# Two transformer blocks on one core: the second block's joints by halves, a shorter opening, one early turn

## What is computed

```python
def rms_norm(x, gain):
    y = x * lax.rsqrt(jnp.mean(x * x, axis=-1, keepdims=True) + NORM_EPS)
    return y * gain

def swiglu_2(h, w_in, w_out):
    g, u = jnp.split(h @ w_in, 2, axis=-1)
    return (jax.nn.silu(g) * u) @ w_out

def second_block(x, ...):
    for layer in range(2):
        g = norm_gain[layer]
        h = swiglu_2(rms_norm(x, g[0]), ffn_w_in[layer, 0], ffn_w_out[layer, 0])
        x = x + 0.5 * rms_norm(h, g[1])
        h = token_mixer(rms_norm(x, g[2]), ...)
        x = x + rms_norm(h, g[3])
        h = swiglu_2(rms_norm(x, g[4]), ffn_w_in[layer, 1], ffn_w_out[layer, 1])
        x = x + 0.5 * rms_norm(h, g[5])
    return x
```

## Time and profile before

| | |
|---|---|
| median of 3 runs | 2106.71 us (2106.12 to 2107.46) |
| the profiled execution | 2107.18 us |
| its span, first to last instruction | 2105.4 us |
| TensorE busy in it | 99% |
| VectorE, ScalarE busy | 80%, 51% |
| DMA moved | 395.56 MB, 188 GB/s |
| granted clock of TensorE | 1.00 |

### The profile page before, as it was taken

The page is one execution under the profiler, slowest core; times in us unless marked ns, Lnnn a source line. Parts: engine busy times, 40 slices in busy tenths (PEclk is TensorE's granted clock), DMA queues, the critical chain, the costliest instruction groups (busy, mean ns, idle before and its releaser), DMA issues.

```text
span 2105.4 us, 28912 instructions
## 1 busy us (share of the span) xinstructions
PE 2093.0 (99%) x10580; PEld 1777.1 (84%) x10580; DVE 1685.9 (80%) x3158; ACT 1082.8 (51%) x1568; POOL 87.0 (4%) x128
## 2 busy tenths in 40 slices
PE   9999999999999999999999999999999999999998
PEld 7888999888888899988878888988888888888887
DVE  5888766888888877778888887779889888678886
ACT  5445553544544455444454446575445445666443
POOL 0000010000000000000000001010000000101000
PEclk9999999999999999999999999999999999999999
DMA  7765755666566584557656767446665765645663
GB/s 243 237 195 173 225 163 161 190 213 197 178 218 195 170 240 146 185 168 226 195 153 212 218 190 196 124 137 209 211 196 171 223 192 169 185 141 162 211 191 106
DMA packets 314368, 395.56 MB, mean 188 GB/s; under 512 B 17972, under 2 KB 272212, under 8 KB 313972
## 3 DMA queue, kind: packets, MB, share of 16 engines
q1 hardware_dynamic: 309120, 375.52, 58.1%
q0 software_dynamic: 4944, 18.14, 2.8%
q10 hardware_dynamic: 164, 0.06, 0.0%
HBM read 392.59 MB, written 1.06 MB: 187 GB/s over the span
## 4 chain that ended last, share of the span: by engine, by line
PE 95%; DVE 2%; ACT 1%; issue 1%; POOL 0%; DMA 0%; DVEq 0%; POOLq 0%; SPq 0%; ACTq 0%
PE bank L310 26%; PE bank L312 26%; PE bank L311 26%; PE bank L304 4%; PE bank L305 4%; PE bank L306 4%; PE bank L491 1%; DVE w_lo L294 1%; PE bank L1472 1%; PE bank L1493 1%; PE bank L1001 1%; PE bank L1564 1%; DVE x L805 0%; ACT w_hi L287 0%; ACT xt_hi L834 0%
## 5 line engine op out<-in xcount | busy, mean ns | idle before, releaser
L287 ACT ACTIVATE w_hi<-stage 128x1024 fp32r<-128x1024 f32 x711 | 747.0, 1058 | 636.3 <-PE bank L312 530.6
L294 DVE TENSOR_TENSOR w_lo<-stage,w_hi 128x1024 fp32r<-128x1024 f32 x711 | 865.5, 1223 | 215.8 <-ACT w_hi L287 208.7
L310 PE MATMUL bank<-w_hi,xt_hi 128*128 128x512 f32 x1760 | 691.4, 393 | 1.7 <-DVE w_lo L621 1.5
L312 PE MATMUL bank<-w_hi,xt_lo 128*128 128x512 f32 x1760 | 685.5, 389 | 0.0
L311 PE MATMUL bank<-w_lo,xt_hi 128*128 128x512 f32 x1760 | 685.2, 389 | 0.0
L477 DVE STREAM_TRANSPOSE hidden<-hidden 32x128 f32<-32x128 f32 (+1 forms) x1376 | 391.7, 285 | 21.3
L310 PEld LDWEIGHTS bank<-w_hi,xt_hi 128*128 128x128 f32 x1760 | 330.5, 188 | 70.1 <-DVE w_lo L621 1.7
L312 PEld LDWEIGHTS bank<-w_hi,xt_lo 128*128 128x128 f32 x1760 | 330.4, 188 | 69.3
L311 PEld LDWEIGHTS bank<-w_lo,xt_hi 128*128 128x128 f32 x1760 | 330.6, 188 | 66.3
L310 PE MATMUL bank<-w_hi,mt_hi 128*128 128x512 f32 x768 | 303.2, 395 | 0.6 <-DVE mt_lo L561 0.6
L312 PE MATMUL bank<-w_hi,mt_lo 128*128 128x512 f32 x768 | 299.4, 390 | 0.0
(11 more groups left out here) (279 smaller groups left out, 1396.5 us busy)
## 6 DMA issues: line engine op xcount, KB each, us to landing
stage<-in_ffn_w SPq DMA_DIRECT2D x352, 256.0 KB, 3.2
stage<-in_ffn_w_in SPq DMA_DIRECT2D x352, 256.0 KB, 3.2
stage<-in_ffn_w SPq DMA_DIRECT2D x88, 512.0 KB, 3.7
stage<-in_ffn_w_out SPq DMA_DIRECT2D x88, 512.0 KB, 3.7
stage<-in_w_in SPq DMA_DIRECT2D x80, 512.0 KB, 4.2
stage<-in_mix_w_in SPq DMA_DIRECT2D x56, 512.0 KB, 4.3
stage<-in_w_out SPq DMA_DIRECT2D x16, 512.0 KB, 4.1
stage<-in_mix_w_out SPq DMA_DIRECT2D x16, 512.0 KB, 3.5
```

The source lines that it names most:

```text
L287: act.activation(w_hi[:, u % RING, :], stage[:, u % STAGED, :], ACT.Copy).then_inc(S["hi_ready"], 1)
L294: dve.tensor_tensor(w_lo[:, u % RING, :], stage[:, u % STAGED, :], f32(w_hi[:, u % RING, :]), ALU.subtract).then_inc(S["lo_ready"], 1)
L310: pe.matmul(o, m_hi, hi, start=first, stop=False)
L312: return pe.matmul(o, m_lo, hi, start=False, stop=last)
```

## The change

Six edits:

1. `WARM` goes from 14 to 8.
2. In stage 0 VectorE turns tile 0's hidden step 2 at units 15 and 16 rather than 16 and 17.
3. At the joints from stage 5 on, x of a tile is made by halves, and each half is followed at once by its product with the next norm's row (`dve_pre_half`).
4. Tile 1's half turns in stages 6, 8, 9 and 11 stand behind tile 0's units 5 and 6 rather than both ahead of unit 5. VectorE's order there: the gate first, then x and product by halves, `xt_lo` of half 0, `w_lo` of unit 6, `xt_lo` of half 1.
5. Tile 0's turns into stage 6: half 0 ahead of tile 1's last unit, half 1 behind it; `xt_lo` by halves round the `w_lo`. Into the other stages both stay ahead of the last unit.
6. The variance behind a stage of the second block: the first half sum is scaled early, and one instruction adds the second.

```diff
-WARM = 14
+WARM = 8
...
-            first = [...] if s else [(16, 2, 18, [(0, 2)])]
+            first = [...] if s else [(15, 2, 17, [(0, 2)])]
...
         def pe_ffn(pe, s):
-                if s and v == LAG - 1:
+                if 0 < s < BLOCK2 and v == LAG - 1:
                     pe_turn_x(pe, s, 1)
                 pe_ffn_tile(pe, s, 0, v)
+                if s >= BLOCK2 and v in (LAG - 1, LAG):
+                    pe_turn_half(pe, s, 1, v - LAG + 1)
...
                 if turn and v == n - 1:
-                    pe_turn_x(pe, s + 1, 0)
+                    pe_turn_half(pe, s + 1, 0, 0)
+                    if s + 1 != BLOCK2:
+                        pe_turn_half(pe, s + 1, 0, 1)
                 pe_ffn_tile(pe, s, 1, v)
                 pe_turn_hidden(pe, s, 1, v)
+            if s + 1 == BLOCK2:
+                pe_turn_half(pe, s + 1, 0, 1)
...
         def dve_ffn(dve, s):
                 lo_upto(dve, b + 6)
-                dve_norm_x(dve, s - 1, 1)
-                dve_pre_x(dve, s, 1)
-                dve_gate(dve, s, 0, 0)
-                lo_upto(dve, b + 7)
-                dve_xt(dve, s, 1)
+                if s >= BLOCK2:
+                    dve_gate(dve, s, 0, 0)
+                    dve_norm_x(dve, s - 1, 1)
+                    dve_xt_half(dve, s, 1, 0)
+                    lo_upto(dve, b + 7)
+                    dve_xt_half(dve, s, 1, 1)
+                else:
+                    dve_norm_x(dve, s - 1, 1)
+                    dve_gate(dve, s, 0, 0)
+                    lo_upto(dve, b + 7)
+                    dve_xt(dve, s, 1)
                 if s >= BLOCK2:
                     dve_pre_var(dve, s, 1)
                 lo_upto(dve, b + 9)
...
         def dve_norm_start(dve, s, t, between=lambda: None):
+                factor = post_factor(s)
+                dve.tensor_scalar(var[:, t:t + 1], ss[:, 2 * t:2 * t + 1], factor ** -2 / D, factor ** -2 * NORM_EPS,
+                                  ALU.mult, ALU.add).then_inc(S["post_half"], 1)
...
         def dve_norm_var(dve, s, t):
-                dve.tensor_tensor(ss[:, 2 * t:2 * t + 1], ss[:, 2 * t:2 * t + 1], ss[:, 2 * t + 1:2 * t + 2], ALU.add)\
-                   .then_inc(S["post_sum"], 1)
-                dve.wait_ge(S["post_sum"], post_at(s, t))
-                dve.tensor_scalar(var[:, t:t + 1], ss[:, 2 * t:2 * t + 1], factor ** -2 / D, factor ** -2 * NORM_EPS,
-                                  ALU.mult, ALU.add).then_inc(S["post_var"], 1)
+                dve.scalar_tensor_tensor(var[:, t:t + 1], ss[:, 2 * t + 1:2 * t + 2], post_factor(s) ** -2 / D,
+                                         var[:, t:t + 1], ALU.mult, ALU.add).then_inc(S["post_var"], 1)
...
         def dve_norm_x(dve, s, t):
-                w = D if s + 1 < len(STAGES) else D // 2
-                for c in range(0, D, w):
-                    dve.scalar_tensor_tensor(x[:, t, c:c + w], r[:, t, c:c + w], rstd[:, t:t + 1], x[:, t, c:c + w],
+                for h in range(2):
+                    c = slice(h * 512, (h + 1) * 512)
+                    dve.scalar_tensor_tensor(x[:, t, c], r[:, t, c], rstd[:, t:t + 1], x[:, t, c],
                                              ALU.mult, ALU.add).then_inc(S["x_ready"], 1)
+                    if s + 1 < len(STAGES):
+                        dve_pre_half(dve, s + 1, t, h, rows[:, 1, :])
...
+        def dve_pre_half(dve, s, t, h, gain):
+
+            c = slice(h * 512, (h + 1) * 512)
+            dve.wait_ge(S["x_ready"], x_at(s - 1, t, h))
+            dve.tensor_tensor(xh[:, t, c], x[:, t, c], gain[:, c], ALU.mult).then_inc(S["pre_x"], 1)
```

More of the change, by code:

```diff
@@ L117, in build @@
                   "ln_resid", "ln_mean", "ln_xg", "ln_ss", "ln_var", "ln_rstd", "x_ready",
-                  "post_ss", "post_scaled", "post_sum", "post_var", "post_rstd",
+                  "post_ss", "post_scaled", "post_half", "post_var", "post_rstd",
                   "pre_ss", "pre_var", "pre_rstd", "pre_x", "x_turned", "xt_hi_out", "xt_lo_out"):
@@ L459, in block_turns @@
         def block_turns(s):
-            first = [(8, 2, 10, [(0, 1)]), (10, 2, 12, [(1, 0)])] if s else [(16, 2, 18, [(0, 2)])]
+            first = [(8, 2, 10, [(0, 1)]), (10, 2, 12, [(1, 0)])] if s else [(15, 2, 17, [(0, 2)])]
             both = [(6 * i + 8, 4, 6 * i + 12, [(0, i + 1), (1, i)]) for i in range(1 if s else 2, STEPS - 2)]
@@ L674, in dve_ffn @@
             if s + 1 < len(STAGES):
-                dve_pre_x(dve, s + 1, 0)
-                lo_upto(dve, b + n + 4)
-                dve_xt(dve, s + 1, 0)
+                if s + 1 == BLOCK2:
+                    dve_xt_half(dve, s + 1, 0, 0)
+                    lo_upto(dve, b + n + 4)
+                    dve_xt_half(dve, s + 1, 0, 1)
+                else:
+                    lo_upto(dve, b + n + 4)
+                    dve_xt(dve, s + 1, 0)
                 if scaled_later(s + 1):
@@ L685, in x_at @@
         def x_at(s, t, h):
-            if s < BLOCK2:
-                return 4 * s + 2 * t + h + 1
-            return 4 * BLOCK2 + 2 * (s - BLOCK2) + (t if s + 1 < len(STAGES) else 2 * t + h) + 1
+            return 4 * s + 2 * t + h + 1
         def x_done(s, t):
@@ L763, in act_norm_sq, with post_factor @@
                        .then_inc(S["post_ss"], 1)
+        def post_factor(s):
+            return 1.0 if STAGES[s] == "mix2" else 0.5
         def dve_norm_var(dve, s, t):
@@ L770, in dve_norm_var @@
             else:
-                factor = 1.0 if STAGES[s] == "mix2" else 0.5
+                dve.wait_ge(S["post_half"], post_at(s, t))
                 dve.wait_ge(S["post_ss"], 2 * post_at(s, t))
-                dve.tensor_tensor(ss[:, 2 * t:2 * t + 1], ss[:, 2 * t:2 * t + 1], ss[:, 2 * t + 1:2 * t + 2], ALU.add)\
-                   .then_inc(S["post_sum"], 1)
-                dve.wait_ge(S["post_sum"], post_at(s, t))
-                dve.tensor_scalar(var[:, t:t + 1], ss[:, 2 * t:2 * t + 1], factor ** -2 / D, factor ** -2 * NORM_EPS,
-                                  ALU.mult, ALU.add).then_inc(S["post_var"], 1)
+                dve.scalar_tensor_tensor(var[:, t:t + 1], ss[:, 2 * t + 1:2 * t + 2], post_factor(s) ** -2 / D,
+                                         var[:, t:t + 1], ALU.mult, ALU.add).then_inc(S["post_var"], 1)
                 if last(s, t):
@@ L799, in dve_norm_x @@
                                              ALU.add).then_inc(S["x_ready"], 1)
+                    if s + 1 == BLOCK2:
+                        dve_pre_half(dve, s + 1, t, h, row3)
             else:
@@ L820, in pool_pre @@
                 .then_inc(S["pre_rstd"], 1)
-        def dve_pre_x(dve, s, t):
-            if s < BLOCK2:
-                return
-            gain = row3 if s == BLOCK2 else rows[:, 1, :]
-            dve.wait_ge(S["x_ready"], x_done(s - 1, t))
-            for h in range(2):
-                c = slice(h * 512, (h + 1) * 512)
-                dve.tensor_tensor(xh[:, t, c], x[:, t, c], gain[:, c], ALU.mult).then_inc(S["pre_x"], 1)
+        def dve_pre_half(dve, s, t, h, gain):
+            c = slice(h * 512, (h + 1) * 512)
+            dve.wait_ge(S["x_ready"], x_at(s - 1, t, h))
+            dve.tensor_tensor(xh[:, t, c], x[:, t, c], gain[:, c], ALU.mult).then_inc(S["pre_x"], 1)
         def act_xt_half(act, s, t, h):
```

2 lines of the change are left out of this document (removed).

## The result

| | before | changed |
|---|---|---|
| median of 5 runs | 2107.17 us (2106.12 to 2107.84) | 2125.82 us (2125.32 to 2128.03) |
| profiled execution | 2107.18 us | 2128.03 us |
| its span | 2105.4 us | 2126.3 us |
| granted TensorE clock, mean of the span | 1.000 | 0.995 |

The change makes the kernel slower: ratio 1.0091, 95% interval [1.0081, 1.0102], +18.65 us in the medians where +14.0 was forecast. The profiled execution is the slowest of the five, +20.9 us; the other four have clocks of 0.996 to 0.998 where it has 0.995.

What follows compares the result with a forecast made beforehand. TensorE, busy 2093.0 of 2105.4 us, was taken as the bound. Terms -1.3 - 0.6 - 0.2 + 0.7 + 0.1 + 17.0 - 2.7 + 1.0 = +14.0 us, on the median 2106.71, gave 2120.7 us; range 2114.5 to 2127.0.

Steps and rivals of the forecast that it cites:

- The pauses of tile 1's joints: Stages 6, 8, 9, 11: TensorE stands 2.5 us, then 1.75 us, for VectorE's low weights, four times: +17.0 us.
- a hidden second pause: Rival, tile 1's joints: unit 7's low weights ready within tile 1's unit 0, only first pause remains; 2113.7 us, chance 0.06.
- weights ahead: Rival, tile 1's joints: low weights of units 6 and 7 made before the half turns, no pauses; 2101.9 us, chance 0.05.
- Given back -2.7: Tile 1's joints: the old waits ahead of these turns go, with 0.11 us each inside a pair: -2.7 us.
- new +1.0: Stages 8 and 11: the gate, now ahead of x, waits for a silu; half 0 is 0.5 us late: +1.0 us.
- Tile 0's joints: Into stages 7, 9, 10: x and product by halves make the second half later, +0.23 us each, +0.7.
- the mixers: Tile 1's joints into stages 7 and 10: the shorter variance takes back the split, +0.1 us in all.
- The early turn: Stage 0: tile 0's single turn and mt_lo one w_lo earlier, removing TensorE's wait for mt_lo: -0.6 us.
- the end: Program's end: one 128x1 step less between the last square and the last rstd: -0.2 us.
- The opening: Kernel's start: fewer products on zeros let tile 0's turns and the first weighted product come sooner: -1.3 us.
- the clock rises late in the opening: Rival, opening: the first weighted products run at the lower clock level, 2.1 us more; 2122.8 us, chance 0.07.
- The clock in the pauses: Rival, tile 1's joints: the clock falls in the pauses, 1.6 us a joint, 6.4 in all; 2127.1 us, chance 0.08.

Runs made afterwards that it cites:

- e4: The change plus nine unused identity products behind the hidden turn, filling the first pause in stages 6, 8, 9 and 11: 2123.3 us, +16.3.
- e5: The kernel before with only the change's order of tile 1's half turns and unit 6's low weights, x whole, 14 zeros: 2124.33 us, +18.0.
- e2: The change, but VectorE makes unit 6's low weights ahead of x, with the gate behind x: 2115.88 us, +8.9.
- e7: The kernel before with only the single turn of stage 0 a unit sooner and the new variance form: 2105.75 us, -0.6.
- e6: The kernel before with only WARM 14 to 8 (8 products on zeros): 2106.23 us over 11 runs, -0.1.
- e12: The change with WARM back at 14 (all 14 products on zeros): 2125.62 us, +18.9.
- e3: The change, but low weights of units 6 and 7 made ahead of both xt_lo of tile 1: 2116.36 us, +9.4.
- e10: e3 with ScalarE's square of tile 1's x and VectorE's step on it moved later: 2110.8 us, +4.1.
- e8: e1 with 14 zeros, and tile 0's half 1 low part and squares put behind the units' weights: 2108.36 us, +2.0.
- e11: The change with TensorE's old order alone (both tile 1 half turns ahead of unit 5), VectorE's order as changed: 2118.33 us, +11.6.
- e1: The change with tile 1's half turns and VectorE's order there as before, x and product still by halves: 2108.96 us, +2.0.

## Why the prediction came out as it did

The measured median lies 5.1 us above the forecast's 2120.7 and inside its range; as a difference to before it is +18.65 for +14.0. The terms can be weighed by the distance of two products that stand on both sides of a joint (start us of each, from the timelines; before, the change, and e4, where the upper level held):

| joint | before | change | e4 |
|---|---|---|---|
| both tiles into stage 6 | 1085.14 to 1110.03 | 1083.97 to 1113.24, +4.4 | 1082.91 to 1110.74, +2.9 |
| tile 1 into stage 8 | 1416.23 to 1430.22 | 1419.83 to 1439.37, +5.6 | 1417.32 to 1435.89, +4.6 |
| tile 1 into stage 9 | 1604.22 to 1616.11 | 1613.60 to 1631.32, +5.8 | 1610.16 to 1626.36, +4.3 |
| tile 1 into stage 11 | 1920.06 to 1936.07 | 1935.67 to 1956.98, +5.3 | 1930.63 to 1951.20, +4.6 |
| sum (forecast 15.3) | | +21.1 | +16.4 |

Term by term:

**The pauses of tile 1's joints (+17.0): right.** The first was worked out at 2.5 us and is 2.49, four times; the second at 1.75 and is 1.82 where TensorE ran at the upper level (1.23 and 0.99 in the stages where the lower one had made tile 1's unit 0 longer and ate part of it). e5 shows that the order alone does it, e2 that the two pauses are two, and the rivals that needed a hidden second pause or weights ahead fell. One piece was left out: the first product behind a pause takes 0.34 us to the next one's start and not 0.23 (1615.12 to 1615.46 and 1620.28 to 1620.61 in e4), eight times, 0.9 us. With 0.07 more for each second pause this is the 1.1 us by which e4's joints exceed the forecast's 15.3 (17.0 - 2.7 + 1.0).

**Given back -2.7, new +1.0: right.** Tile 1's x is late by 0.53 and 0.48 us in stages 8 and 11, behind the silu and the gate, as forecast. In stage 6 tile 0 starts 0.66 sooner and tile 1 loses 0.38 and 0.32: nothing, as forecast.

**Tile 0's joints (+0.23 each): right; the mixers (+0.1): too small.** Between the products on both sides of tile 0's turns the change adds 0.25, 0.25 and 0.23 us into stages 7, 9 and 10. Tile 1 into the mixers adds 0.13 and 0.15, +0.3 in all for +0.1: the split cost more there than the shorter variance took back. Here the waits inside VectorE's chain cost what the row said, 0.1 us. "VectorE: DVE Perf Modes" of the Trainium skill, section "The DRAIN you can't avoid", says that the semaphore costs nothing extra; the trace differs: x starts 0.77 us before its product (1613.80 and 1614.57), where two steps like it with no wait between, at the program's end, take 1.41 us and so start 0.67 apart.

**The early turn (-0.6) and the end (-0.2): right in kind.** The mt_lo wait is gone; its missing issue time was 0.8 us rather than 0.6 (from 58.31 to 59.33, less 0.23). At the end one 128x1 step stands for two, and the time from the last product's start to the end of the span falls from 6.12 to 6.00, 0.1 us. e7 measures -0.6 for both, and its interval holds no change. That the shorter opening takes the same mt_lo wait away (e6) the forecast did not see: the two terms are not independent.

**The opening (-1.3): the first step that failed.** The chain moved further than worked out (the forecast had the first product at 7.9; it came at 7.41, because the turns at 4.54 took 0.63 us where 1.04 was counted), but the term took for granted that the clock would be up at the weighted products behind the shorter zeros. In the changed kernel's profile 0.25 is left, e6 gives -0.1 over 11 runs, and the change less e12 -0.2. The forecast named a rival of this kind, "the clock rises late in the opening", at 0.07, with a worse price (+2.1). Of the eight profiles with 8 zeros two show it (products 0.43 us apart up to 13 us, e3 and e10); in three, the change's among them, the clock fell again behind the stand ahead of the first product, and in three it stayed up. A lower level in the opening should have been the likeliest case for that term, since the rows showed the clock rising only some 4.4 us after the first product, and the edit ends the zeros at about that point. The section "PE-mode transpose" of "TensorE: Matmul & The Clock Gate" in the Trainium skill says that turns don't count as activity, and by it the stretch of turns and standing is one long gap. The traces bear that out in part at most: in three of eight the clock stayed up through it, and no run parts the turns from the standing. "Part 1: The HAM clock gate" on the same page says that how long a kernel begins at the lower level varies from run to run; the eight values of e6's section agree, from 14.68 to 17.65.

**The clock in the pauses: the second step that failed.** Given 0.08 as a rival, with 1.6 us a joint. It came about: 0.43 us between products in four joints of the profiled execution, where the table has 4.7 us more for the change than for e4. That is 1.2 a joint and not 1.6: the six products and the turns did cost some 1.5 us more, but in stages 8 and 11 the second pause was shorter by 0.59 and 0.83, because the slower unit ahead of it had used up a part. The price was near and the chance too low. "Why this matters for your kernels" on the same page warns of idle gaps between bursts, but of longer ones than this; here 2.3 us of idle had 0.50 behind it, and the measurement decides. But it is not each pause in each execution: in the median run it costs 2.4 us by e4.

**The sum again, for the median:** 14.0, + 1.2 (opening), - 0.2 (early turn), + 0.1 (end), + 0.2 (mixers), + 1.1 (the pauses at the upper level), + 2.4 (clock, from e4) = +18.8, of a measured +18.65. The range held the result although two terms failed, because together these are 3.6 us and the range reached 6.3 above the forecast.

What stays open is which pause is followed by the lower level. Pauses of 2.49 us were followed by it four times of four in the change, once of four in e12 and never of three in e5 (one profiled execution of each); the 1.93 of e5, the 2.21 of e8 and three of e11's four waits in two parts were, e1's like them in stage 6 (1.69 and 0.90) was not; seventeen second pauses of 1.75 or 1.82 us in the change, e2, e4, e5 and e12 were not. The length alone doesn't say it. Nor does it begin at once: in e12's stage 6 the products from 1103.41 to 1104.22 still stand as at the upper level, and the lower one begins behind them. No run was made that changes only what stands ahead of a pause.

## What to carry to other kernels

Splitting a transfer between engines by halves paid in no run here: not where TensorE took both halves in a row (e1), and not where it had a unit to do between them (e5, e8). Before such a split, ask what else stands in the producers' queues behind the second half. Here each half turn began a chain across two engines, and the next unit's weights were queued behind it in a fixed order; write such chains out from the queue's order, link by link, and they can be priced: the two pauses came out within 0.1 us. Any edit that opens a stand of some two microseconds in TensorE, or shortens what keeps it busy before the first product, should be given a clock term of its own. Of the thirteen stands of 1.9 us or more in mid-kernel that nothing filled (the change, e5, e8 and e12) seven were followed by the lower level, so a chance near even is fair; products in the gap, whose result nobody uses, test it.

## What the runs showed of the hardware

- The same kernel's pauses of the same length were followed by TensorE's lower level or not: four of four (change), one of four (e12). Where it fell it stayed for 3.4 us of the trace. It cost 1.2 us a joint, measured against e4.
- Nine products of an identity, 18 records in 2.17 us, in a pause of 2.49 us delayed nothing, and the upper level held in all four joints (e4). In the same kernel without them it held in none (the change), with 14 zeros in three of four (e12), so a part of that can be chance.
- The first product behind a wait takes 0.34 us to the next one's start at the upper level, where the following ones take 0.23 (e4, 1615.12 to 1615.46 and then to 1615.70).
- The printed PEclk is not the whole story in the opening. In e10's profile products of 512 columns are 0.43 us apart up to 13.08, and the window over them prints 1.00 (two views, the timeline and the windows):

```profile
8.22 0.79 PE L310 MATMUL bank<-w_hi,xt_hi 128*128 128x512 f32 x1
8.81 0.63 PE L311 MATMUL bank<-w_lo,xt_hi 128*128 128x512 f32 x1
...
13.08 0.60 PE L312 MATMUL bank<-w_hi,xt_lo 128*128 128x512 f32 x1
```
```profile
8.00:13.00 5.00, 5.00 (x14) 1.00 1.07 364
```

The distance of the starts shows the level that the clock was really at: the lower.
